# Squares of the k and q norms in a rounded part and a remainder: two fp32r products in place of one fp32 product

## The reference, cut to what matters

```python
def l2n(x):
    return x * lax.rsqrt(jnp.sum(x * x, -1, keepdims=True) + EPS)
...
    conv = sum(buf[:, j:j + t_len] * cw[j] for j in range(CONV_W))
    conv = jax.nn.silu(conv)
    cq, ck, cv = jnp.split(conv, 3, axis=-1)
    o_gd, S1_gd = gdn_scan(l2n(heads(cq)) * HEAD_DIM ** -0.5, l2n(heads(ck)), heads(cv),
                           beta, logg, S0_gd.astype(f32))
```

## Time and profile before

| what | value |
|---|---|
| median of 3 runs | 2353.14 us (2348.16 to 2358.45) |
| the profiled execution's own time | 2351.84 us |
| its span | 2350.0 us |
| mean granted clock of TensorE | 0.972 |
| TensorE matmuls busy | 2216.7 us, 94% of the span |
| VectorE, ScalarE, GpSimd busy | 906.4, 804.1, 665.9 us |

### The profile page before, as it was taken

How to read it: one execution, slowest core, us unless ns; L and a number is a source line. 1 busy time by engine, 2 the same in 40 slices (tenths; PEclk the granted TensorE clock), 3 DMA queues, 4 the chain that set the end, 5 groups by cost and what they waited for, 6 DMA issues and landing times.

```text
span 2350.0 us, 36727 instructions
## 1 busy us (share of the span) xinstructions
PE 2216.7 (94%) x14000; PEld 2153.8 (92%) x14000; DVE 906.4 (39%) x1361; ACT 804.1 (34%) x1442; POOL 665.9 (28%) x469
## 2 busy tenths in 40 slices
PE   4999999999999899999999799979999999999997
PEld 3999999999789899899998798979999999999997
DVE  5687332322473644144333356333221211212215
ACT  4365323232354554133331233224123132232232
POOL 1348622321443533211112122211212212222221
PEclk9999999999899999999997899999999999999999
DMA  4223646442324233246441554310111101111112
GB/s 157 60 71 108 183 135 162 132 126 73 101 73 143 67 108 101 76 134 185 144 125 38 186 173 140 107 64 19 59 40 45 58 28 52 54 30 54 49 36 88
DMA packets 193055, 222.51 MB, mean 95 GB/s; under 512 B 40078, under 2 KB 147634, under 8 KB 192854
## 3 DMA queue, kind: packets, MB, share of 16 engines
q1 hardware_dynamic: 169884, 181.91, 25.8%
q10 hardware_dynamic: 23098, 39.60, 4.6%
HBM read 162.22 MB, written 59.25 MB: 94 GB/s over the span
## 4 chain that ended last, share of the span: by engine, by line
PE 79%; DVE 10%; issue 3%; POOL 3%; DMA 2%; ACT 2%; SPq 1%; DVEq 0%; ACTq 0%; POOLq 0%
PE D L373 68%; DVE g_dq L915 1%; DVE m_rd L1971 1%; PE M L814 1%; DVE xn_lo L2191 1%; POOL b_t L678 1%; POOL b_u L675 1%; POOL w_lo L354 1%; DVE u_x L487 1%; PE M L1752 1%; DVE g_lg L1103 1%; DVE acc L2186 0%; PE M L2084 0%; ACT g_sg L846 0%; PE M L2115 0%
## 5 line engine op out<-in xcount | busy, mean ns | idle before, releaser
L373 PE MATMUL D<-xn_hi,w_hi 128*128 128x352 f32 x2808 | 942.4, 336 | 60.3 <-DVE xn_lo L2191 23.4
L373 PE MATMUL D<-xn_hi,w_lo 128*128 128x352 f32 x2808 | 913.9, 325 | 0.0
L373 PE MATMUL D<-xn_lo,w_hi 128*128 128x352 f32 x2808 | 913.1, 325 | 0.0
L373 PEld LDWEIGHTS D<-xn_hi,w_hi 128*128 128x128 f32 x2808 | 537.6, 191 | 84.3 <-issue 38.5
L373 PEld LDWEIGHTS D<-xn_lo,w_hi 128*128 128x128 f32 x2808 | 539.2, 192 | 4.7 <-issue 3.8
L373 PEld LDWEIGHTS D<-xn_hi,w_lo 128*128 128x128 f32 x2808 | 536.6, 191 | 0.0
L354 POOL TENSOR_TENSOR w_lo<-w_raw,w_hi 128x1024 fp32r<-128x1024 f32 (+1 forms) x105 | 246.3, 2345 | 674.5 <-ACT w_hi L348 674.5
L354 POOL TENSOR_TENSOR w_lo<-e,w_hi 128x512 fp32r<-128x512 f32 (+1 forms) x96 | 163.8, 1706 | 608.0 <-ACT w_hi L348 608.0
L373 PE MATMUL D<-y_hi,w_hi 128*128 128x352 f32 x960 | 311.9, 325 | 18.0 <-DVE y_lo L2260 14.6
L373 PE MATMUL D<-y_lo,w_hi 128*128 128x352 f32 x960 | 311.8, 325 | 0.0
L373 PE MATMUL D<-y_hi,w_lo 128*128 128x352 f32 x960 | 311.3, 324 | 0.0
(11 more groups left out here) (442 smaller groups left out, 2331.4 us busy)
## 6 DMA issues: line engine op xcount, KB each, us to landing
w_raw<-in_w_proj SPq DMA_DIRECT2D x73, 512.0 KB, 3.8
proj<-stage ACTq DMA_DIRECT2D x61, 528.0 KB, 2.8
e<-in_w_full SPq DMA_DIRECT2D x32, 512.0 KB, 3.6
e<-in_w_half SPq DMA_DIRECT2D x64, 256.0 KB, 2.6
stage<-proj SPq DMA_DIRECT2D x24, 528.0 KB, 3.6
d_bc<-rowd SPq DMA_DIRECT2D x32, 256.0 KB, 5.7
m_in<-proj SPq DMA_DIRECT2D x32, 256.0 KB, 3.9
proj<-u_o SPq DMA_DIRECT2D x12, 528.0 KB, 2.9
```

What stands on the lines that cost most here:

```text
L373: last = nc.tensor.matmul(D[b][:, 0:GN], w[t.slot][:, k, :], x[:, k, cols], start=(k == 0 and n == 0), stop=(k == kt - 1 and n == 2))
```

## The change

The square of tile c is followed on ScalarE by a copy that rounds it to fp32r (`u_qh`). VectorE subtracts the rounded part from the square, in place, as fp32r (`u_ql`, which lies where `u_q` lies). This new step stands behind `qn` of tile c - 1 in VectorE's queue, ahead of `inverse_decay` and of the taking out of the blocks. The product of ones is then made of two fp32r products for each column group, which are summed in the same bank, and it waits for the subtraction in place of the square. The ones are copied once to fp32r, by ScalarE, ahead of the first norm.

```diff
+            arena(a, "u_gap1", [P, 16180 - 10 * T - 16])
+            u_qh = arena(a, "u_qh", [P, T], F32R)
+            ones_r = arena(a, "ones_r", [P, P], F32R)
+        with ExitStack() as a:
+            arena(a, "ul_gap", [P, 4 * T + 2 * CONV_LEN + 2 * T])
+            u_ql = arena(a, "u_ql", [P, T], F32R)
...
                 eng.activation(u_q[:, :], o, ACT.Square).then_inc(*cv_act.step(f"q{c}"))
+                eng.wait_ge(*cv_act.after(f"q{c}"))
+                eng.activation(u_qh[:, :], u_q[:, :], ACT.Copy).then_inc(*cv_act.step(f"y{c}"))
+            if op == "ql":
+                eng.wait_ge(*cv_act.after(f"y{c}"))
+                eng.tensor_tensor(u_ql[:, :], u_q[:, :], u_qh[:, :].bitcast(F32), ALU.subtract).then_inc(*cv_dve.step(f"y{c}"))
             if op == "nq":
-                eng.wait_ge(*cv_act.after(f"q{c}"))
+                eng.wait_ge(*cv_dve.after(f"y{c}"))
                 if c:
                     eng.wait_ge(*cv_act.after(f"w{c - 1}"))
+                else:
+                    eng.wait_ge(ones_made, 1)
                 for g in range(TG):
-                    i = eng.matmul(M[3 + g][:, 0:GN], ones, u_q[:, cols(g)], start=True, stop=True)
+                    eng.matmul(M[3 + g][:, 0:GN], ones_r[:, :], u_qh[:, cols(g)], start=True, stop=False)
+                    i = eng.matmul(M[3 + g][:, 0:GN], ones_r[:, :], u_ql[:, cols(g)], start=False, stop=True)
                 i.then_inc(*cv_pe.step(f"n{c}"))
...
                     if 0 < c <= NORMED:
                         post("qn", c - 1)
+                    if c < NORMED:
+                        post("ql", c)
                     if c == 1:
                         inverse_decay(kind, eng)
...
+            act.wait_ge(const_ld, 32)
+            act.activation(ones_r[:, :], ones, ACT.Copy).then_inc(ones_made, 1)
             for k in range(KT):
```

More of the change, by code:

```diff
@@ L412, in silu_names @@
             return f"s{c} t{c}"
-        cv_dve = steps("cv_dve", " ".join([conv_names(0)] + [(conv_names(c + 1) + " " if c + 1 < NCONV else "") + silu_names(c) + (f" n{c - 1}" if 0 < c <= NORMED else "")
+        cv_dve = steps("cv_dve", " ".join([conv_names(0)] + [(conv_names(c + 1) + " " if c + 1 < NCONV else "") + silu_names(c) + (f" n{c - 1}" if 0 < c <= NORMED else "") + (f" y{c}" if c < NORMED else "")
                                                              for c in range(NCONV)]))
-        cv_act = steps("cv_act", " ".join(f"e{c} l{c} s{c}" + (f" u{c - 1} v{c - 1} w{c - 1} r{c - 1}" if 0 < c <= NORMED else "") + (f" q{c}" if c < NORMED else "")
+        cv_act = steps("cv_act", " ".join(f"e{c} l{c} s{c}" + (f" u{c - 1} v{c - 1} w{c - 1} r{c - 1}" if 0 < c <= NORMED else "") + (f" q{c} y{c}" if c < NORMED else "")
                                           for c in range(NCONV)))
@@ L420, in build @@
         cv_pe = steps("cv_pe", " ".join(f"n{c}" for c in range(NORMED)))
+        ones_made = sem("ones_made")
         cv_st = [sem(f"cv_st{s}") for s in range(2)]
```

## The result

| | before | changed |
|---|---|---|
| median of 20 runs | 2352.32 us (2347.20 to 2360.59) | 2364.36 us (2357.47 to 2370.41) |
| ratio of the means | 1 | 1.0048, 95% interval 1.0037 to 1.0059 |
| span of the profiled execution | 2350.0 us | 2358.4 us |
| mean granted clock in it | 0.972 | 0.971 |

The changed kernel is slower by 12.0 us at the median; the ratio makes it 11.3 us (8.7 to 13.9). Forecast were 2362, range 2352 to 2370. The profiled execution shows 8.4 us in its span.

The account below looks back on a forecast made before the run. TensorE was 94% busy, but the chain also ran through VectorE and GpSimd. Blocks 10.0 us later, elimination 1.0 more and the last tiles' clock regained gave +9.1: 2360.9 for the profiled execution, 2362 at the median, range 2352 to 2370.

Parts of the forecast that it names:

- hop, tile 0 ready to remainder: Convolution stage: square, rounding copy and subtraction follow each other by semaphores, 3.55 us from tile ready to remainder ready.
- P(1), P(2), P(3) with the drop: Full-pitch starts of TensorE's dense products in iterations 1 to 3: 108.3, 123.2, 143.4 us, the last plus 1.9 for the clock.
- price of that drop: Lower TensorE clock behind the long wait for head 0's blocks in iteration 2: 1.9 us more, added once.
- a round of the loop: Iterations 3 to 5, from dense products through norm, square, copy, subtraction and blocks to the next dense products: 15.56 us, before 15.01.
- the price of one more meeting with VectorE: GpSimd's elimination: subtractions of tiles 6 and 7 added, one `qn` gone, costing GpSimd 1.0 us, bounds 0 and 2.0.
- The prediction's other estimate for it: GpSimd's elimination: by the Trainium skill's SBUF rule the two subtractions cost 2.5 us instead of 1.0, making the sum +10.6.
- The wait of iteration 7: TensorE's products of ones wait 1 to 2 us for the subtraction in this iteration, as in iterations 0 and 6.
- the prediction's only shorter wait: Kernel before: a TensorE wait just under 1 us ahead of 134.52, which left no trace in the 11.45 us behind it.
- (a): Convolution stage: the waits are hidden and TensorE's whole saving of 6.6 us stands, 2346.6 us; chance 0.04.
- (b): Iteration 2's stall doesn't lower the clock, and GpSimd gains from VectorE's idleness: +5 us, 2358; chance 0.22.
- (c): TensorE's short stalls or the last one at `w_lo` also lower the clock: +1.9 to +3.8 us more, 2365; chance 0.20.
- (d): The fp32r products of ones don't run at the dense pitch: +3.3 us, 2365; chance 0.06.

Follow-up runs that it names:

- filled wait: Changed kernel plus 34 unread fp32r products in TensorE's wait of iteration 2; ratio 1.0037 against the kernel before, +8.7 us.
- split kernels: Changed kernel with the subtraction after the blocks and two fp32r products only for tiles 2 to 7 or 2 to 4, fp32 elsewhere; ratios 1.0010 and 0.9996 against before.
- hop alone: Changed kernel with copy, subtraction and waits kept, but one fp32 product of the rounded squares; ratio 1.0059 against the kernel before, +13.9 us.
- products alone: Changed kernel without copy and subtraction: square writes fp32r, rounded squares summed twice, waits of the kernel before; ratio 0.9970 against that kernel, -7.1 us.
- split of tiles 2 to 4: Changed kernel with the subtraction after the blocks and two fp32r products only for tiles 2 to 4, fp32 elsewhere; ratio 0.9996 against before, -0.9 us.

## Why the prediction was right, and where it was off

The course through the iterations came as worked out:

| step of the prediction | forecast, us | measured, us |
|---|---|---|
| saving of the products, tile | 0.82 | 0.81 (6 in 0.96, where nothing waits, for 1.77) |
| hop, tile 0 ready to remainder | 3.55 | 3.53 (103.73 to 107.26) |
| P(1), P(2), P(3) with the drop | 108.3, 123.2, 145.3 | 108.38, 123.33, 144.61 |
| blocks of head 0 out | 140.3 | 140.04 |
| wait of TensorE before k k^T | 5.7 | 5.40, and the drop of the clock behind it |
| price of that drop | 1.9 | 1.6 (filled wait) |
| a round of the loop | 15.56 | 15.7 |
| blocks of head 3 out | 188.85 | 188.64 |
| `w_lo` of the last but two iterations | 257.3 | 255.8 |
| the last two dense tiles, as the clock no longer falls in them | -1.9 | -1.6 |
| scan starts later by | 9.1 | 7.9 (7.9 and 8.0 from the common start) |

The mechanism was right; three terms were off in size. The blocks came back from memory in 197.79 - 188.64 = 9.15 us, not 9.8. GpSimd's elimination up to that `w_lo` took 58.0 us where it had taken 57.6: the price of one more meeting with VectorE was 0.4 here and not 1.0 (between the two split kernels, which differ by three subtractions, three copies and their products, 1.1 for the whole elimination). The prediction's other estimate for it, 2.5, was not met either: 0.4 is the net of all that changed there, with one `qn` less. And the execution as timed lost more than the stage: 9 to 11 us against the 8 that both traces show at the scan's start. These misses have opposite signs, 1.2 us too much at the scan and 1 to 3 too little behind it, so that they partly cancel in the total of 2362 against 2364.4: that much was luck.

The drop of the clock at the last stalls came as forecast, one tile earlier than before (0.57 at 242 to 246 us, then 1.00 to the end of the stage), and was covered by GpSimd. That was in part luck too: waits of this length brought the clock down in some executions and not in others (last section), and in hop alone the drop fell on the last two tiles. Of the signs named, one failed: TensorE's busy time in the line of the products did not fall by 6 to 7 us, for the reason given above (16.1 against 15.5). The wait of iteration 7 was 0.46 us, not 1 to 2. And the prediction's only shorter wait, ahead of 134.52, was 0.66 us; it overlooked one of 0.77 ahead of 231.69.

**Rivals.** (a), that the waits are hidden and the whole saving stands, is out: the changed kernel is slower. In the traces the saving is worth 1.3 to 1.6 us at the blocks even without the hop or with the hop hidden (products alone, both split kernels), though the timed products alone leave room for more. (b), no second price of the clock, is out: it was there, and filling the wait took it away. (c), that short stalls cost clock, is out for this stage: behind every wait of up to 1.68 us TensorE ran at 1.00. But its size, 2365, was nearly met for another reason, which is not found: 2.2 us of it go with the lower mean clock of a typical execution, by the working above. (d) is out: the products ran at the dense pitch.

**What was the cause.** Not the added busy time as such, but the hop where nothing covers it: with the same copies and subtractions for tiles 2 to 7, the last blocks come 11.5 us earlier relative to the stage's start than in the changed kernel, and 1.6 before those of the kernel before. Moving the subtraction behind the blocks gives 5.0 of the 11.5; leaving tiles 0 and 1 alone, which takes their hops out and doesn't move them, gives 6.5.

## What to carry to other kernels

A cheaper product is worth what lies on the chain, here about 1.6 of 6.6 us by the traces, while each new hand-off is paid by every engine that stands in it: price the hop (3.5 us), not the busy time (1.25), and ask what is queued behind the waiting instruction. Put a subtraction that only a later product needs last in its engine's iteration, and leave out the first iterations, in which nothing covers it. When a wait is moved, look where it turns up next: two of the four moves tried here made a new one. And where one stage is changed, compare traces from a common start within it: what follows scatters by several us.

## What the runs showed of the hardware

TensorE's waits between 100 and 265 us in the ten profiles, and the granted clock in the 7 us behind each:

| wait, us | how many | clock behind it |
|---|---|---|
| 0.18 to 1.68 | 40 | 1.00 behind all |
| 2.05 to 2.31 | 3 | 1.00 behind all |
| 2.33 to 2.99 | 13 | down to 0.50 behind eight (2.33 three times, 2.47, 2.66, 2.89, 2.91, 2.99), 1.00 behind five (2.54, 2.67, 2.69, 2.81, 2.83) |
| 4.35 and 5.40 | 4 | down to 0.50 behind all |

So in this kernel a wait between 2.33 and 2.99 us may or may not bring the clock down, and its length within that stretch doesn't say which. It happens at one and the same place: ahead of the last two dense tiles the kernel before waited 2.91 us and then ran at 0.62 in 248 to 252 us, the split of tiles 2 to 4 waited 2.83 us and ran at 1.00 there.

```profile
246.88 0.43 PE L379 MATMUL D<-xn_hi,w_hi 128*128 128x352 f32 x1 [2.83 <-POOL w_lo L360]
```

```profile
248.00:252.00 4.00, 4.00 (x27) 4.00 (x26) 1.80 (x2) 1.80 (x3) 3.61 (x6) 1.00 0.85 257
```

27 matmuls fit in those 4 us, 18 before. On the chain such a drop cost 1.1 to 1.6 us in the last two tiles (25.8 and 25.9 us with it, 24.3 to 24.7 in the eight executions without). Within each kernel the time of an execution falls as its mean clock rises; whether kernels with more waits of this length scatter more is not shown.

VectorE's instructions with two inputs in SBUF and GpSimd's hold each other up in both directions: 3.41 us for 1.26 on VectorE's side, 1.53 for 0.52 on GpSimd's. The Trainium skill, page "SBUF — State Buffer", section "Who interferes with whom", has whichever starts first block the other for the whole instruction. The trace agrees, since the subtraction ended 1.12 us after GpSimd's instruction. VectorE's multiplication by a constant, with one input, was held up too, 2.83 us for 0.70, and ended 0.54 us after GpSimd's (123.99 and 123.45).
